# Router weights shared between VectorE and GpSimd, and both parts of the input in one matmul of the up projection

## What is computed

```python
def hier_moe(x, ...):
    probs_g = softmax(xf @ w_group + b_group)
    p_top, g_idx = top_k(probs_g, 1)
    in_group = take(xf @ w_router + b_router, g_idx)      # 4 logits
    w_top, e_local = top_k(softmax(in_group), 2)
    w_top = w_top / sum(w_top)
    gates = p_top * w_top at the two experts
    h = silu(x @ w_gate[e]) * (x @ w_up[e])
    y = sum over e of (h * gates[e]) @ w_down[e]

def conv_ffn(x, w_up, conv_w, conv_b, w_down):            # FFN_DIM = 2816
    u, g = split(x @ w_up, 2)
    g = causal_dwconv(g, conv_w, conv_b)                  # 3 taps
    return (gelu(g) * u) @ w_down
```

## Time and profile before

| | |
|---|---|
| median of three runs | 1001.53 us (1001.23 to 1001.97) |
| the profiled execution | 1001.3 us, span 999.6 us |
| DVE, ACT, POOL busy | 714.7, 549.8, 31.3 us |
| expert layers (about) | 190 to 346 us and 482 to 638 us |
| up projection | 779.8 to 906.7 us |
| down projection | 908.3 to about 960 us |
| largest waits of PE, by cause | `xt_lo` 4.6, `w_lo` 2.8, issue 2.8 us |

### The profile page before, as it was taken

How to read it: one execution, slowest core, us unless ns; L and a number is a source line. 1 busy time by engine, 2 the same in 40 slices (tenths; PEclk the granted TensorE clock), 3 DMA queues, 4 the chain that set the end, 5 groups by cost and what they waited for, 6 DMA issues and landing times.

```text
span 999.6 us, 15243 instructions
## 1 busy us (share of the span) xinstructions
PE 966.7 (97%) x5906; PEld 840.2 (84%) x5906; DVE 714.7 (72%) x891; ACT 549.8 (55%) x608; POOL 31.3 (3%) x73
## 2 busy tenths in 40 slices
PE   8999989999999999999999999899999999999997
PEld 8978988878888789878778888689887999998886
DVE  4788877888888774536989888845566766566566
ACT  3765644567677644653677677434553644444431
POOL 7000010000000000000000000000000000000010
PEclk9999999999999999999999999999999999999999
DMA  9653325299899945521599899736351755554611
GB/s 322 212 170 126 127 72 185 86 364 348 295 328 350 357 145 167 170 85 43 170 357 349 271 344 361 264 115 200 131 189 63 244 177 168 185 193 169 234 61 43
DMA packets 151987, 205.86 MB, mean 206 GB/s; under 512 B 6896, under 2 KB 123376, under 8 KB 151920
## 3 DMA queue, kind: packets, MB, share of 16 engines
q1 hardware_dynamic: 150912, 204.24, 60.8%
q10 hardware_dynamic: 1008, 0.71, 0.2%
HBM read 203.87 MB, written 1.05 MB: 205 GB/s over the span
## 4 chain that ended last, share of the span: by engine, by line
PE 73%; DVE 11%; ACT 6%; DMA 5%; issue 4%; SPq 0%; POOL 0%; ACTq 0%; POOLq 0%; DVEq 0%
PE psum L619 70%; DVE w_lo L1900 5%; ACT w_hi L1460 3%; DMA raw<-in_w_up 3%; DMA raw<-in_w_down 1%; ACT arena L1460 1%; DMA raw<-in_attn_w_in 1%; DVE stats L2147 1%; DVE x_res L2167 1%; DVE xt_lo L1917 1%; DVE mt_lo L1917 1%; ACT mt_hi L1460 0%; PE psum L1094 0%; PE psum L1345 0%; ACT L1460 0%
## 5 line engine op out<-in xcount | busy, mean ns | idle before, releaser
L1900 DVE TENSOR_TENSOR w_lo<-raw,w_hi 128x2048 fp32r<-128x2048 f32 x184 | 417.7, 2287 | 79.5 <-ACT w_hi L1460 74.5
L1460 ACT ACTIVATE w_hi<-raw 128x2048 fp32r<-128x2048 f32 (+1 forms) x186 | 353.6, 1905 | 127.5 <-PE psum L619 61.8
L619 PE MATMUL psum<-xt_hi,w_hi 128*128 128x256 f32 x704 | 200.9, 285 | 3.7 <-DVE xt_lo L1917 1.6
L619 PE MATMUL psum<-xt_hi,w_lo 128*128 128x256 f32 x704 | 199.2, 283 | 0.0
L619 PE MATMUL psum<-xt_lo,w_hi 128*128 128x256 f32 x704 | 199.1, 283 | 0.0
L619 PE MATMUL psum<-w_hi,mt_hi 128*128 128x512 f32 (+1 forms) x448 | 174.3, 389 | 2.9 <-DVE arena L2612 1.5
L619 PE MATMUL psum<-w_hi,mt_lo 128*128 128x512 f32 (+1 forms) x448 | 171.3, 382 | 0.0
L619 PE MATMUL psum<-w_lo,mt_hi 128*128 128x512 f32 (+1 forms) x448 | 171.0, 382 | 0.0
L619 PEld LDWEIGHTS psum<-xt_hi,w_hi 128*128 128x128 f32 x704 | 135.0, 192 | 5.1 <-issue 4.8
L619 PEld LDWEIGHTS psum<-xt_hi,w_lo 128*128 128x128 f32 x704 | 135.1, 192 | 0.0
L619 PEld LDWEIGHTS psum<-xt_lo,w_hi 128*128 128x128 f32 x704 | 135.0, 192 | 0.0
(11 more groups left out here) (261 smaller groups left out, 1196.6 us busy)
## 6 DMA issues: line engine op xcount, KB each, us to landing
raw<-in_w_gate SPq DMA_DIRECT2D x64, 512.0 KB, 5.1
raw<-in_w_up SPq DMA_DIRECT2D x64, 512.0 KB, 6.2
raw<-in_w_down SPq DMA_DIRECT2D x64, 512.0 KB, 5.8
raw<-in_ffn_w_up SPq DMA_DIRECT2D x44, 512.0 KB, 4.6
raw<-in_a_w_in SPq DMA_DIRECT2D x26, 512.0 KB, 6.8
raw<-in_attn_w_in SPq DMA_DIRECT2D x24, 512.0 KB, 5.2
raw<-in_ffn_w_down SPq DMA_DIRECT2D x22, 512.0 KB, 4.2
raw<-in_w_o SPq DMA_DIRECT2D x16, 512.0 KB, 4.7
```

The source lines that it names most:

```text
L619: return pe.matmul(o, l, r, start=start, stop=stop, skip_group_check=skip)
L1460: return act.activation(o, i, f, **kw)
L1900: return dve.tensor_tensor(w_half(h, w_lo), w_half(h, raw), w_half(h, w_hi).bitcast(F32), ALU.subtract).then_inc(lo_split, 1)
```

## The change

1. `xt_hi` and `xt_lo` become the two halves of one tile `xt`. In the up projection each rounded weight tile takes both of them in one matmul of 512 columns; the rest of the weight takes `xt_hi` in one of 256, added to the first half of the same bank. One block c now fills a whole bank, a pair fills four and two pairs all eight. The two halves of a bank have to be added: ACT copies the second half of each to the tile `mixed` (`low_part`) and DVE adds the first (`both_parts`), once for g and once for u. Scaling, taps and product then read `mixed`. PE waits for `pp_out` before the loop.
2. `weigh_experts` moves to POOL, except the two searches for the largest (`first_pick`, `second_pick`), which stay on DVE. They hand over to each other by semaphores: `expert_logits`, `first_pick`, `others_left`, `second_pick`, `gated`. `second_pick` stands after DVE's first split in the first group; ACT's `expert_log` now comes from POOL.

```diff
-        xt_hi = sb("xt_hi", [P, KC, T], F32R)
-        xt_lo = sb("xt_lo", [P, KC, T], F32R)
+        xt = sb("xt", [P, 2, KC, T], F32R)
+        xt_hi, xt_lo = xt[:, 0, :, :], xt[:, 1, :, :]
...
+            def weigh_experts(layer):
+
+                m = [r_m[:, n, :].rearrange("p (b o) -> p b o", o=1) for n in range(8)]
+                chosen = r_og.rearrange("p b (g o) -> p b g o", o=1).to_broadcast([P, 2, 4, 4])
+                pool.wait_ge(sem("group_ready"), layer + 1)
+                own.link(pool.tensor_tensor(r_t16, r_log[:, :, 4:20].rearrange("p b (g e) -> p b g e", g=4),
+                                            chosen, ALU.mult))
+                own.link(pool.tensor_tensor(r_t16[:, :, 0:2, :], r_t16[:, :, 0:2, :], r_t16[:, :, 2:4, :], ALU.add))
+                pool.tensor_tensor(r_i4, r_t16[:, :, 0, :], r_t16[:, :, 1, :], ALU.add)\
+                    .then_inc(sem("expert_logits"), 1)
+
+                pool.wait_ge(sem("first_pick"), layer + 1)
+                pool.tensor_tensor(r_e, r_i4, m[4].to_broadcast([P, 2, 4]), ALU.subtract)\
+                    .then_inc(sem("expert_log"), 1)
+                pool.wait_ge(sem("group_exp"), layer + 1)
+                own.link(pool.tensor_tensor(r_w2, r_g[:, :, 0:2], r_g[:, :, 2:4], ALU.add))
+                own.did(pool.tensor_tensor(m[2], r_w2[:, :, 0:1], r_w2[:, :, 1:2], ALU.add))
+                pool.wait_ge(sem("expert_exp"), layer + 1)
+                own.link(pool.tensor_tensor(r_e2, r_e, r_o1, ALU.subtract))
+                pool.tensor_tensor(r_e2, r_e2, r_o1, ALU.subtract).then_inc(sem("others_left"), 1)
+
+                pool.wait_ge(sem("second_pick"), layer + 1)
+                one = ones[:, 0:2].rearrange("p (b o) -> p b o", o=1)
+                own.did(pool.tensor_tensor(r_o1, r_o1, r_o2, ALU.add))
+                own.link(pool.tensor_tensor(m[7], m[6], one, ALU.add))
+                own.did(pool.tensor_tensor(r_g4, r_e, r_o1, ALU.mult))
+                own.link(pool.tensor_tensor(m[7], m[7], m[2], ALU.mult))
+                own.link(pool.tensor_tensor(m[7], m[7], neg_ones[:, 0:2].rearrange("p (b o) -> p b o", o=1), ALU.pow))
+                own.link(pool.tensor_scalar(m[7], m[7], 1.0 / ALPHA, None, ALU.mult))
+                own.link(pool.tensor_tensor(r_g4, r_g4, m[7].to_broadcast([P, 2, 4]), ALU.mult))
+                own.link(pool.tensor_tensor(r_gate, r_g4.rearrange("p b (o e) -> p b o e", o=1)
+                                            .to_broadcast([P, 2, 4, 4]), chosen, ALU.mult))
+                pool.nop().then_inc(sem("gated"), 1)
...
-            for _ in range(6):
+            for turn in range(6):
                 for b in range(TB):
                     n += 1
                     power(n, slice(b, b + 1))
+                if turn in (0, 2):
+                    weigh_experts(turn // 2)
...
                 for q in range(2):
                     pe.wait_ge(lo_split, h + q + 1 if i is None else i * 4 + (h + q + 1))
-                    fm_products(h + q, 2 * (j % 2) + q, xt_hi, xt_lo)
+                    wh, wl = (w_half(h + q, w).rearrange("p (k n) -> p k n", k=8) for w in (w_hi, w_lo))
+                    for c in range(2):
+                        o, ws = psum[:, 4 * (j % 2) + 2 * q + c, :], slice(P * c, P * c + P)
+                        for k in range(KC):
+                            mm(o, wh[:, k, ws], xt[:, :, k, :], k == 0, False, skip=True)
+                            last = mm(o[:, 0:T], wl[:, k, ws], xt_hi[:, k, :], False, k == KC - 1, skip=True)
+                    last.then_inc(half_used, 1)
+
+            pe.wait_ge(sem("pp_out"), 1)
...
+                def low_part(at_col, q):
+
+                    v = psum[:, 4 * (j % 2) + 2 * q:4 * (j % 2) + 2 * q + 2, T:2 * T]
+                    o = mixed[:, j % 2, at_col:at_col + 512].rearrange("p (c t) -> p c t", c=2)
+                    return fn(o, v, ACT.Copy)
+
+                low_part(0, 0).then_inc(sem("ff_low"), 1)
+                act.wait_ge(sem("ff_sum"), at(j + 1, 2))
...
-                    last = fn(ff_t[:, j % 2, T * c:T * c + T], psum[:, 2 * (j % 2), T * c:T * c + T],
+                    last = fn(ff_t[:, j % 2, T * c:T * c + T], mixed[:, j % 2, T * c:T * c + T],
                               ACT.Identity, bias=bb, scale=w2)
...
                 fn(ff_g[:, j % 2, :], ff_t[:, j % 2, :], ACT.Gelu).then_inc(sem("ff_gelu"), 1)
+                act.wait_ge(half_used, at(h + 2, 4))
+                low_part(512, 1).then_inc(sem("ff_val_low"), 1)
...
-            def weigh_experts(layer):
-
-                own.link(dve.tensor_tensor(
-                    r_t16, r_log[:, :, 4:20].rearrange("p b (g e) -> p b g e", g=4),
-                    r_og.rearrange("p b (g o) -> p b g o", o=1).to_broadcast([P, 2, 4, 4]), ALU.mult))
-                own.link(dve.tensor_reduce(r_i4, r_t16
...
+            def first_pick(layer):
+
+                dve.wait_ge(sem("expert_logits"), layer + 1)
                 own.link(dve.tensor_reduce(r_m[:, 4, :], r_i4, AX, ALU.max))
-                dve.tensor_tensor(r_e, r_i4, wide(r_m[:, 4, :]), ALU.subtract).then_inc(sem("expert_log"), 1)
                 first_of(r_o1, r_i4, r_m[:, 4, :])
...
+                dve.nop().then_inc(sem("first_pick"), 1)
+
+            def second_pick(layer):
+
+                dve.wait_ge(sem("others_left"), layer + 1)
                 own.link(dve.tensor_reduce(r_m[:, 6, :], r_e2, AX, ALU.max))
                 first_of(r_o2, r_e2, r_m[:, 6, :])
...
+                dve.nop().then_inc(sem("second_pick"), 1)
...
                     if q == 0 and not dense:
+                        if i == 0:
+                            spl(3)
+                            second_pick(layer)
                         spl(6)
                         slot_gates()
...
                 gather(0)
-                weigh_experts(layer)
+                first_pick(layer)
...
+                def both_parts(at_col, q):
+
+                    v = psum[:, 4 * (j % 2) + 2 * q:4 * (j % 2) + 2 * q + 2, :]
+                    o = mixed[:, j % 2, at_col:at_col + 512].rearrange("p (c t) -> p c t", c=2)
+                    return dve.tensor_tensor(o, o, v[:, :, 0:T], ALU.add)
...
+                dve.wait_ge(sem("ff_low"), at(j + 1, 2))
+                both_parts(0, 0).then_inc(sem("ff_sum"), 1)
                 dve.wait_ge(sem("ff_mid"), at(j + 1, 2))
...
-                        last = dve.scalar_tensor_tensor(o, psum[:, 2 * (j % 2), T * c:T * c + T - lag], w, o,
+                        last = dve.scalar_tensor_tensor(o, mixed[:, j % 2, T * c:T * c + T - lag], w, o,
...
+                dve.wait_ge(sem("ff_val_low"), at(j + 1, 2))
+                both_parts(512, 1).then_inc(sem("ff_val"), 1)
+                dve.wait_ge(sem("ff_val"), at(j + 1, 2))
...
-                dve.tensor_tensor(fa.rearrange("p k t -> p (k t)"), ff_g[:, j % 2, :], psum[:, 2 * (j % 2) + 1, :],
+                dve.tensor_tensor(fa.rearrange("p k t -> p (k t)"), ff_g[:, j % 2, :], mixed[:, j % 2, 512:1024],
```

More of the change, by code:

```diff
@@ L416, in _ @@
             sp.wait_ge(out_in, 16 * len(GATE_TILES))
+        r_log = rt[:, 0:40].rearrange("p (b e) -> p b e", b=2)
+        r_g = rt[:, 40:48].rearrange("p (b e) -> p b e", b=2)
+        r_eq = rt[:, 48:56]
+        r_cum = rt[:, 56:64]
+        r_og = rt[:, 64:72].rearrange("p (b e) -> p b e", b=2)
+        r_t16 = rt[:, 72:104].rearrange("p (b g e) -> p b g e", b=2, g=4)
+        r_e = rt[:, 104:112].rearrange("p (b e) -> p b e", b=2)
+        r_o1 = rt[:, 112:120].rearrange("p (b e) -> p b e", b=2)
+        r_o2 = rt[:, 120:128].rearrange("p (b e) -> p b e", b=2)
+        r_m = rt[:, 128:144].rearrange("p (n b) -> p n b", b=2)
+        r_g4 = rt[:, 144:152].rearrange("p (b e) -> p b e", b=2)
+        r_gate = rt[:, 160:192].rearrange("p (b g e) -> p b g e", b=2, g=4)
+        r_pos = rt[:, 192:204].rearrange("p (n g) -> p n g", g=4)
+        r_i4 = rt[:, 208:216].rearrange("p (b e) -> p b e", b=2)
+        r_e2 = rt[:, 216:224].rearrange("p (b e) -> p b e", b=2)
+        r_mx = rt[:, 224:225]
+        r_w2 = rt[:, 228:232].rearrange("p (b e) -> p b e", b=2)
         @block.gpsimd
@@ L2316, in place_slots @@
                 place(layer, None)
-            def weigh_experts(layer):
-                own.link(dve.tensor_tensor(
-                    r_t16, r_log[:, :, 4:20].rearrange("p b (g e) -> p b g e", g=4),
-                    r_og.rearrange("p b (g o) -> p b g o", o=1).to_broadcast([P, 2, 4, 4]), ALU.mult))
-                own.link(dve.tensor_reduce(r_i4, r_t16.rearrange("p b g e -> p b e g"), AX, ALU.add))
+            def first_pick(layer):
+                dve.wait_ge(sem("expert_logits"), layer + 1)
                 own.link(dve.tensor_reduce(r_m[:, 4, :], r_i4, AX, ALU.max))
-                dve.tensor_tensor(r_e, r_i4, wide(r_m[:, 4, :]), ALU.subtract).then_inc(sem("expert_log"), 1)
                 first_of(r_o1, r_i4, r_m[:, 4, :])
[L2328 to L2333, removed]
```

(21 more changed lines are left out.)

18 lines of the change are left out of this document (1 added, 17 removed).

## The result

| | before | changed |
|---|---|---|
| runs beside each other, median (lowest to highest) | 1001.97 us (1001.23 to 1002.94) | 1016.11 us (1014.64 to 1018.91) |
| ratio, 95% interval | | 1.0147 (1.0128 to 1.0166) |
| profiled execution | 1001.3 us | 1014.64 us, span 1012.9 us |

What follows compares the result with a forecast made beforehand. The prediction took TensorE, busy 97% of the span, as the bound. It summed -4.9 + 1.75 + 3.8 + 7.4 = +8.05 us on the profiled 1001.3 us and, adjusted to the median, forecast 1009.5 us, range 999.5 to 1014.5.

Steps and rivals of the forecast that it cites:

- Step 1: Up projection: one 512- and one 256-column matmul replace three of 256 in 352 steps; 4.9 us less.
- Step 2: Start of the up projection: PE waits for `pp_out`, ACT's two copies out of banks 4 to 7; 1.75 us more.
- Step 3: Inside the up loop: added ACT copies and DVE additions stay covered by PE's work; no change.
- Step 4: Before the down projection: draining pair 10, with DVE's splits ahead of the additions, makes PE wait 5.5 us; 3.8 more.
- Step 5: Router in both expert layers: DVE's splits hold POOL, so the gates come late; 3.7 us more each, 7.4 together.
- scenario A: The main forecast, with POOL held by DVE's splits in the router: 1009.5 us; chance 0.50.
- rival B: PE's clock falls behind its long waits, 1.8 us a fall, one to three falls: 1011.3 to 1015 us; chance 0.18.
- C: Router: POOL is not held by splits, gates arrive before PE, layers gain 2.4 us: 999.8 us; chance 0.10.
- D: POOL not held in the router and a short tail, 1.3 instead of 3.8 us: 997.3 us; chance 0.09.
- E: Router: POOL half held, gates 1 to 2 us late instead of 4.2: 1003.2 to 1005.2 us; chance 0.13.

Runs made afterwards that it cites:

- e9: The changed kernel run again, unaltered, beside the kernel before: 1016.18 us, ratio 1.0136.
- e12: e6 with its 512-column matmul taken apart into two of 256 on the same weights: 1002.74 us, ratio 1.0006.
- e13: e6 run once more, unaltered, as comparison for e12: 999.66 us, ratio 0.9976.
- e10: Changed up projection, old router, `pp_out` wait behind the first pair, DVE's two splits of pair 10 behind its last product: 1000.91 us, ratio 0.9989.
- e4: Changed kernel with one added wait: DVE waits for `gated` before its next three splits. 1009.39 us, ratio 1.0074.
- e8: Changed kernel with the router operations behind `second_pick` moved from POOL back to DVE, as seven, ahead of the three splits: 1004.58 us, ratio 1.0022.
- e3: Changed kernel with PE's four long waits filled by matmuls on zeros: 1006.08 us, ratio 1.0045.
- e6: Changed up projection, old router, `pp_out` wait behind the first pair, pair 10 in its old form: 1000.31 us, ratio 0.9982.
- e7: The router of e8 together with the start and tail of e6: 998.76 us, ratio 0.9971.

## Why the prediction was wrong, step by step

The sign, the places and nearly all waits were right; the sum was short by 5.3 us in the profiled execution and 6.6 in the median, because each long wait was priced at its own length.

*Step 1, wider matmuls* (forecast -4.9): a step took 0.3467 us in the first profile and in e9, as forecast, so in these executions the term was right. But it is one of two values: 352 steps save 4.7 us at 0.3467 and 2.3 at 0.3533. The medians of e12 and e13, 3.1 us in 320 steps and so 3.4 in 352, lie between them. The rival rule was N/2.4 ns plus 2.5 ns (the Trainium skill, "TensorE: Matmul & The Clock Gate", section "Back-to-back issue gap"), which that section gives for a matmul by itself and calls too low for small N where each matmul has its weight load; by it the step would save 0.9 us in all. As a price for this stream the trace disagrees with it: 6.7 or 13.3 ns a step, not 2.5.

*Step 2, the start* (+1.75): +1.85, the first matmul 0.45 us after the second copy. Right.

*Step 3, nothing inside the loop:* right; PE is busy without a gap from 795 to 914 us.

*Step 4, the tail* (a wait of 5.5, +3.8): 5.40, +3.9. The last DVE rows stand as worked out, the split directly before the last addition; e10 confirms that it is their order. Right.

*Step 5, the router* (+3.7 a layer): GpSimd passes one operation a split, scenario A. PE read the gates 3.3 and 2.9 us late, less the 0.5 that goes at the turn: 2.8 and 2.4. The mechanism is right (e4, e8), the size was 2.2 too high in both layers together: the splits ended 0.5 us earlier than I had them, and behind the last one POOL needed 1.8 us for what was left, not 2.1 to 2.6, having got one operation done ahead of the first split (196.18).

*What failed* is the sum's silent step: each wait was counted at its length, and rival B, which adds the clock, got 0.18 at 1.8 us a fall for "one to three falls". It was four, of 1.7 to 2.9 us. e3 puts their price at 10 us, the rows at 9.0. B with four falls would have said 1016.7, next to the 1016.1 measured, but by luck: 1.8 us a fall is 1.8 too little for the four, and the router's term was 2.2 too high. I had written that no wait in those rows was longer than 1.55 us and that nothing there showed what 5 us do, and still let the forecast go by it; yet the earlier trace rows showed that PE runs slowly from a standstill. The Trainium skill ("TensorE: Matmul & The Clock Gate", section "What's actually happening") says that the engine goes back to 1.2 GHz when it idles; the trace agrees at all four waits, with a granted clock of 0.53 to 0.57 behind them. Without the clock the sum of the measured terms is -4.9 + 1.85 + 3.9 + 2.8 + 2.4 = +6.1; with 9.0 it is 15.1, and the small differences elsewhere (+0.3 - 0.6 - 1.5: waits that are gone and slightly faster streaming) leave the 13.3 seen.

Rivals C, D and E are refuted: each lets two or more of POOL's operations through beside the splits, and it is one per split in both layers; nor were the gates 1 to 2 us late, as E had them, but 3.3 and 2.9.

## What to carry to other kernels

A new wait of TensorE of 2 us or more costs its length and then, nearly always here, 1.7 to 2.9 us more for matmuls at half clock: add about 2 us to each, or fill it with idle matmuls that end inside it. A chain of small GpSimd operations on SBUF must not lie beside VectorE operations with two SBUF operands: three links here took the length of a split each (2.1 to 2.3 us), while VectorE does the same work in 0.2 us apiece. Where a drain gets an operation more, first look what stands in front of it in the queue of the engine that does it; the order was worth 2.7 us, the operations 1.2.

## What I had not expected of the hardware

A fall of the clock needs no wait of 4 us: it came behind 1.98 us (e4), 2.72 (e10) and 2.2 (e6, 0.62 in the 3.4 us behind it). The length of the wait does not decide it alone. In e7 and in e13 PE waits 2.12 us before the down projection; what follows is at full clock in e7 and at half in e13:

```profile
903.80:907.30 3.50, 3.43 (x15) 1.00 0.84 284
908.00:911.50 3.50, 3.43 (x8) 0.51 0.89 293
```

In the fourteen profiles PE has 23 waits of 1.98 us or more, and the clock fell with 22 of them; with the shorter ones, up to 1.73 us, it never did. The fall also does not start with the wait's end: in e10 two matmuls are still fast, in e4 five.

A matmul of 512 columns with an operand in two pieces takes 391 or 399 ns in the records, by the execution, both at a granted clock of 1.00; that is 2 us in the up stage, 122.0 to 122.4 or 124.4 to 124.6 in the profiles without a slow start. The loop of 256 columns showed 126.68 or 126.69 us in all three. What separates the two lengths stays open.
